# A two-layer decoder trunk: expert panels of 1,792 features, expert 0 gathered first, down weights in longer runs

## The reference, cut to what matters

```python
def swiglu(x, w_gate, w_up, w_down):
    return (jax.nn.silu(x @ w_gate) * (x @ w_up)) @ w_down

def moe_swiglu(x, w_router, w_gate, w_up, w_down):
    logits = (x @ w_router).astype(jnp.float32)
    top_vals, top_idx = lax.top_k(logits, TOP_K)          # TOP_K = 2
    weights = jax.nn.softmax(top_vals, axis=-1)
    ...                                                    # combine: weights by expert
    for e in range(N_EXPERTS):                             # 8, each 1024 x 3584 (x 3)
        out = out + combine[..., e:e + 1] * swiglu(x, w_gate[e], w_up[e], w_down[e])
    return out
...
        h = layer_norm(ALPHA * h + f, ln_g[i, 1], ln_b[i, 1])
        h = h + jax.nn.sigmoid(h @ ple_w_gate[i] + ple_b_gate[i]) * (p[i] @ ple_w_proj[i])
```

## Time and profile before

| | |
|---|---|
| median of 3 runs | 1474.14 us (1472.51 to 1475.07) |
| profiled execution, as timed | 1470.26 us |
| its span | 1468.5 us |
| TensorE (PE) busy | 1412.5 us, 96% |
| VectorE busy | 702.5 us, 48% |
| ScalarE busy | 319.8 us, 22% |
| GpSimd busy | 24.6 us, 2% |
| DMA | 467.99 MB, mean 319 GB/s; 130,864 packets on SyncE's queue q1 |
| ring products, gate and up (L1781) | 5,632 instructions |
| ring products, down (L1781) | 3,472 instructions |
| SiLU (L1054), hidden product (L1699) | 88 each, of 224 columns |
| turns (L1707) | 352, of 224 columns |

### The profile page before, as it was taken

The page is one execution under the profiler, slowest core; times in us unless marked ns, Lnnn a source line. Parts: engine busy times, 40 slices in busy tenths (PEclk is TensorE's granted clock), DMA queues, the critical chain, the costliest instruction groups (busy, mean ns, idle before and its releaser), DMA issues.

```text
span 1468.5 us, 27721 instructions
## 1 busy us (share of the span) xinstructions
PE 1412.5 (96%) x12131; PEld 925.5 (63%) x12131; DVE 702.5 (48%) x1128; ACT 319.8 (22%) x432; POOL 24.6 (2%) x51
## 2 busy tenths in 40 slices
PE   8999999999999999999999999999999999999687
PEld 7888788888778877356666664456454454465135
DVE  4795678878874668432332332241422322323247
ACT  4444344344455553000000000000000000000012
POOL 3010000000000000000000000000000000000100
PEclk9999999999999999999999999999999999999998
DMA  9956445555456126999999999999999999999980
GB/s 367 337 197 248 165 172 183 189 200 185 166 177 207 50 78 262 419 412 404 416 414 419 420 419 420 419 418 421 419 419 420 419 420 419 420 420 415 417 348 30
DMA packets 135481, 467.99 MB, mean 319 GB/s; under 512 B 8524, under 2 KB 9376, under 8 KB 134848
## 3 DMA queue, kind: packets, MB, share of 16 engines
q1 hardware_dynamic: 130864, 450.92, 77.9%
q0 software_dynamic: 2992, 12.70, 2.3%
q10 hardware_dynamic: 1504, 2.62, 0.5%
HBM read 462.53 MB, written 3.67 MB: 317 GB/s over the span
## 4 chain that ended last, share of the span: by engine, by line
PE 78%; DMA 13%; DVE 5%; ACT 2%; issue 1%; SPq 1%; POOL 0%; ACTq 0%; POOLq 0%; DVEq 0%
PE ps L1781 76%; DMA ring<-in_moe_w_up_dram 10%; DMA ring<-in_moe_w_down_dram 2%; DMA raw<-in_ple_w_gate_dram 1%; DVE split L1121 1%; PE ps L1799 1%; ACT split L751 1%; DVE h L1169 1%; DVE stats L1173 1%; DVE acc L1164 1%; DVE htl L1136 0%; SPq L578 0%; PE ps L2116 0%; PE ps L2152 0%; DVE acc L1216 0%
## 5 line engine op out<-in xcount | busy, mean ns | idle before, releaser
L1781 PE MATMUL ps<-ring,xt 128*32 128x448 f32 x5632 | 546.2, 542 | 25.9 <-DMA ring<-in_moe_w_up_dram 25.6
L1781 PEld LDWEIGHTS ps<-ring,xt 128*32 128x32 f32 x5632 | 256.7, 110 | 300.0 <-issue 242.1
L1781 PE MATMUL ps<-split,hth 128*128 128x512 f32 x1168 | 366.7, 395 | 6.0 <-DVE htl L1136 2.8
L1699 DVE TENSOR_TENSOR m_hb<-ps,m_sg 128x224 f32<-128x224 f32 x88 | 29.2, 385 | 575.8 <-ACT m_sg L1054 575.8
L1781 PE MATMUL ps<-ring,m_bt 128*32 128x256 f32 (+1 forms) x3472 | 278.4, 469 | 6.8 <-DMA ring<-in_moe_w_down_dram 6.7
L1781 PEld LDWEIGHTS ps<-split,hth 128*128 128x128 f32 x1168 | 218.9, 190 | 53.8 <-DVE htl L1136 3.4
L1781 PEld LDWEIGHTS ps<-ring,m_bt 128*32 128x32 f32 x3472 | 173.0, 110 | 108.7 <-issue 28.8
L1781 PE MATMUL ps<-split,htl 128*128 128x512 f32 x584 | 229.3, 393 | 0.0
L1707 DVE STREAM_TRANSPOSE m_bt<-m_hb 32x224 f32<-32x224 f32 x352 | 205.1, 583 | 5.5
L1054 ACT ACTIVATE m_sg<-ps 128x224 f32<-128x224 f32 x88 | 25.4, 357 | 727.7 <-PE ps L1781 727.7
L1121 DVE TENSOR_TENSOR split<-raw,split 128x2048 fp32r<-128x2048 f32 x52 | 118.7, 2291 | 64.0 <-ACT split L751 63.9
(11 more groups left out here) (256 smaller groups left out, 651.1 us busy)
## 6 DMA issues: line engine op xcount, KB each, us to landing
ring<-in_moe_w_gate_dram SPq DMA_DIRECT2D x128, 896.0 KB, 17.2
ring<-in_moe_w_up_dram SPq DMA_DIRECT2D x128, 896.0 KB, 16.6
ring<-in_moe_w_down_dram SPq DMA_DIRECT2D x128, 896.0 KB, 16.2
raw<-in_gm_w_in_dram SPq DMA_DIRECT2D x14, 1024.0 KB, 14.6
raw<-in_ffn_w_gate_dram SPq DMA_DIRECT2D x14, 1024.0 KB, 5.0
raw<-in_ffn_w_up_dram SPq DMA_DIRECT2D x14, 1024.0 KB, 5.0
raw<-in_ffn_w_down_dram SPq DMA_DIRECT2D x14, 1024.0 KB, 5.0
raw<-in_fox_w_in_dram SPq DMA_DIRECT2D x12, 1024.0 KB, 4.9
```

What stands on the lines that cost most here:

```text
L1699: ins = nc.vector.tensor_tensor(m_hb[:, q, :], ps[bank][:, QTR:2 * QTR], m_sg[:, q, :], ALU.mult)
L1781: return nc.tensor.matmul(o, a, b, start=start, stop=stop)
```

## The change

Panels have 1,792 features: 16 blocks, 24 slots each, one slot now holding one 128-row piece of gate or of up in one run of 7,168 bytes. All eight pieces of gate come first and then all eight of up, in banks of their own, 448 columns wide, and each slot is freed by itself. The up products of a wide panel use bank 0 of the gate products, after SiLU. A down transfer fills two slots in one run of 14,336 bytes and has a semaphore of its own. The order of blocks is expert 0 (2), three wide, one narrow, three wide, one narrow, four wide, two narrow. The hidden product is written over `m_sg`, `m_bt` has one buffer (and another for the last block), and so SiLU waits for the turns of the block before, and the turns wait for the down products of the block before.

`xh` and `xl` have room outside the ring and are made during routing. Expert 0's one-hot is made from `slots_e` before the sort, its gather (32 products of 96 columns) goes first, and the rest of the gather follows gate and up of block 0. The first 16 slots are filled in the order of `FILL`, the last three wait for `lg_full` only. Behind the experts the four gate pieces have a part of `split1` each, ScalarE's casts stand between the norm's steps, GpSimd takes the differences, the Sqrt table is loaded ahead, and the gate products go tile by tile. Code for a second round changes alike and is left out. In the diff `gate_rest` is GpSimd's, `wait_ge(bt_ready, ...)` is ScalarE's ahead of SiLU of block b, `select_first` and `turn_hidden` are VectorE's, `gate_up` and `gather_rest` TensorE's.

```diff
-PANEL = 896
+PANEL = 1792
...
-    SLOT = 2 * PANEL
-    X_BLK = 12
+    SLOT = PANEL
+    X_BLK = 24
...
-        between = len(few) - (NPAN - 1)
+        between = len(few) - NPAN
...
+    FIRST_BANKS = (3, 5)
+    REST_BANKS = (2, 3, 5)
+    def gate_banks(b):
+        return (0, 1) if narrow(b) else (0, 1, 4)
+    def up_banks(b):
+        return (6, 7) if narrow(b) else (6, 7, 0)
...
-    ADD_AT = {len(ORDER) - 2: (0, 1), len(ORDER) - 1: (2, 3)}
+    ADD_AT = {len(ORDER) - 1: (0, 1, 2, 3)}
...
+    FILL = (0, 1, 2, 3, 4, 5, 10, 11, 12, 6, 7, 8, 9, 13, 14, 15)
...
-                sp.wait_ge(gx_full, 2 * KD)
+                sp.wait_ge(lg_full, T)
...
+        for n in FILL:
+            ring_space(n)
             ring_load(n)
+        sp.wait_ge(placed, 1)
+        find_experts()
+        for n in range(RING, N_RING):
+            if not second_half(n):
+                sp.wait_ge(streams[0]["used"], G_MOE + n - RING + (2 if second_half(n + 1) else 1))
+            ring_load(n)
...
+                    if n == down_at(b) + 2 * i:
+                        sp.dma_start(ring[:, slot:slot + 2].rearrange("p (a s) n -> p a (s n)", a=1),
+                                     expert_rows(moe_w_down, e, j, i))                            .then_inc(down_landed[i] if b < NB - 1 else landed, 16)
...
+        def gate_rest(n):
+            pool.wait_ge(streams[1]["hi"], n + 1)
+            pool.tensor_tensor(split1[:, n, 1], raw[:, n], split1[:, n, 0].bitcast(F32), ALU.subtract)\
+                .then_inc(streams[1]["lo"], 1)
...
+                if b or r is not None:
+                    act.wait_ge(bt_ready, hid0 + b)
...
+        nc.scalar.activation(std[:, 0:1], var[:, 0:1], ACT.Sqrt)
         unfold_last()
-        round_hi(0, 1)
-        round_hi(1, 1)
+        gate_hi(0)
         norm_sqrt(1, 0, 1)
+        gate_hi(1)
+        gate_hi(2)
         tile_hi(0, 1)
-        round_hi(2, 1)
         norm_sqrt(1, 1, 1)
+        gate_hi(3)
         tile_hi(1, 1)
-        ple(1, 0, 3, 4)
+        last_ple()
...
+        def select_first(slot):
+            for m in range(T):
+                ins = nc.vector.tensor_scalar(every[:, m, 0, :], iota[:, 0:CAP], slot(m), None, ALU.is_equal)
+            ins.then_inc(every_ready, 1)
...
             def turn_hidden(b):
                 dve.wait_ge(e_hid, hid0 + (b + 1))
+                if 0 < b < NB - 1:
+                    dve.wait_ge(s0["used"], used0 + (G_MOE + down_at(b - 1) + 8))
...
             def gate_up(b):
+                for which, banks in enumerate((gate_banks(b), up_banks(b))):
+                    for k in range(KD):
+                        slot = landed(b, gu_at(b) + which * KD + k)
                         for q, bank in enumerate(banks):
+                            if which == 1 and k == 0 and bank in gate_banks(b):
+                                pe.wait_ge(e_silu, silu0 + (3 * b + gate_banks(b).index(bank) + 1))
                             for t in range(4):
...
+                                last = mm(ps[bank][t * G3:(t + 1) * G3, 0:QTR], xt[:, e // 4, k, tok:tok + G3],
+                                          ring[:, slot, quarter * QTR:(quarter + 1) * QTR], k == 0, k == KD - 1)
+                        last.then_inc(s0["used"], 1)
...
                     gate_up(b)
+                    if b == 0:
+                        pe.wait_ge(route_ready, 1)
+                        gather_rest(at_e, gx0)
```

More of the change, by code:

```diff
@@ L732, in _ @@
             gather_rows(2 * T, 1 + TABLE - CUT)
+        for n in range(4):
+            gate_rest(n)
     @block.scalar
@@ L891, in projected, with ple @@
                     .then_inc(proj_copied, 1)
-        def ple(which, g0, ready, last):
-            st = streams[which]
+        def ple(g0, ready, last):
+            st = streams[0]
             for nb in range(2):
@@ new lines, in ple @@
+                part = slice(nb * W, (nb + 1) * W)
+                dve.wait_ge(st["used"], g0 + 2 + 2 * nb)
+                for m in range(T):
+                    nc.vector.tensor_tensor(sig[:, m, part], ps[2 * (1 - nb) + m][:, :], ple_b[:, 0, part], ALU.add)\
+                        .then_inc(st["gb"], 1)
+                for m in range(T):
+                    dve.wait_ge(st["gs"], nb * T + m + 1)
+                    seq(nc.vector.tensor_tensor(sig[:, m, part], sig[:, m, part], pp[:, m, part], ALU.mult))
@@ new lines, in gather_expert_0 @@
+        def gather_expert_0(x_at, at_e):
+            pe.wait_ge(xh_ready, x_at)
+            pe.wait_ge(xl_ready, x_at)
+            pe.wait_ge(every_ready, at_e)
+            for k in range(KD):
+                o = ps[FIRST_BANKS[k // 4]][:, k % 4 * CAP:(k % 4 + 1) * CAP]
+                for x in (xh, xl):
+                    for m in range(T):
+                        last = mm(o, x[:, m, k * P:(k + 1) * P], every[:, m, 0, :], x is xh and m == 0,
+                                  x is xl and m == T - 1)
+                if k % 4 == 3:
+                    last.then_inc(gx_full, 1)
@@ new lines, in gather_rest @@
+        def gather_rest(at_e, gx0):
+            for n in range(2 * KD):
+                half, k = n // KD, n % KD
+                if k == 0:
+                    pe.wait_ge(every_ready, at_e + (half + 1))
+                if n >= 3:
+                    pe.wait_ge((gx_act, gx_dve)[(n - 3) % 2], gx0 + (2 + (n - 3) // 2))
+                e0 = 4 * half if half else 1
+                o = ps[REST_BANKS[n % 3]][:, 0:(4 * half + 4 - e0) * CAP]
+                for x in (xh, xl):
+                    for m in range(T):
+                        one = every[:, m, e0:4 * half + 4, :].rearrange("p e s -> p (e s)")
+                        last = mm(o, x[:, m, k * P:(k + 1) * P], one, x is xh and m == 0, x is xl and m == T - 1)
+                last.then_inc(gx_full, 1)
```

460 lines of the change are left out of this document (210 added, 250 removed).

## The result

The changed kernel takes 1484.45 us (median of 4 runs, 1483.52 to 1486.01), the kernel before on the same chip 1474.61 (4 runs, 1472.51 to 1475.67): ratio 1.0068, 95% interval 1.0053 to 1.0083. It is 10 us slower. The forecast was 1464.4, with 1459 to 1476 as the range and 0.12 for slower: wrong, and on the wrong side. The profiled execution took 1483.97 us, its span is 1482.2 where the forecast said 1458.8.

The account below looks back on a forecast made before the run. It took TensorE to set the pace up to the first narrow panel and the DMA from there to the last weight; -5.6 us (last slot earlier) and -4.1 (tail) summed to -9.7, median 1464.4, range 1459 to 1476.

Parts of the forecast that it names:

- Tail: From the last slot's products to the end: 4.1 us gained, with GpSimd taking the differences at 4.4 us each.
- R3: Rival, no change: a GpSimd difference takes 6.6 us, the fourth comes 7.2 us late; median 1471.6; chance 0.08.
- Head: Routing to block 0: expert 0's gather starts at 573.2 and takes 4.1 us; gate products begin at 578.1, before at 584.02.
- First narrow panel: Expert stage, after five wide panels: starts at 842.3; at the old pace the last slot is used 3.8 us later.
- The landing: Time from a ring transfer's issue to its arrival, at the first narrow panel: 6.5 us, between 4.6 and 8.3.
- Rate: Weight transfers from the first narrow panel on: longer runs save 0.0366 us a slot, 9.4 us over 256 slots.
- R2: Rival, no change: the weights' transfer rate doesn't move and landing stays at 8.3 us; median 1475.6; chance 0.14.
- Panels: Wide panels: VectorE's 12 turns take 14.0 us at 1.17 each, hidden behind TensorE's work, 4.8 us to spare.
- R1: Rival, slower: VectorE's turns don't fit in the wide panels; at 1.95 us each, 18.4 us, median 1482.8; chance 0.12.

Follow-up runs that it names:

- tail_dve: The changed kernel with the four differences of the last gate weights on VectorE between the token tiles, none on GpSimd: 1477.78 us, 1.0035 of the kernel before.
- both: The changed kernel with the differences back on VectorE (tail_dve) and 58 filler products (warm): 1471.04 us, 0.9990 of the kernel before.
- warm: The changed kernel with 58 instead of 26 filler products ahead of the wait for the experts' membership: 1477.02 us, 1.0033 of the kernel before.
- before_pool: The kernel before, with only the four differences of the last gate weights moved from VectorE to GpSimd: 1479.36 us, 1.0045 of the kernel before.
- gate3584: The kernel both, with each gate and up slot issued as two transfers in runs of 3,584 bytes: 1478.42 us, 1.0042 of the kernel before.
- down7168: The kernel both, with each two-slot down transfer issued as two of one slot, 7,168 bytes per run: 1473.57 us, 1.0004 of the kernel before.
- best: The kernel both with early2's panel order, hybrid's differences, and tile 1's turns behind all tile 0 gate products with more filler: 1460.42 us, 0.9914.
- early2: The kernel both, with the narrow panels as blocks 1, 6, 14 and 15 instead of 5, 9, 14 and 15: 1463.16 us, 0.9933 of the kernel before.
- hybrid: The kernel both, with the first and fourth difference on GpSimd beside VectorE's sums out of PSUM: 1470.76 us, 0.9988 of the kernel before.
- early: The kernel both, with the narrow panels as blocks 1, 6, 11 and 15 instead of 5, 9, 14 and 15: 1472.06 us, 0.9999 of the kernel before.
- newton: The changed kernel, with the last norm's Newton step as three VectorE instructions with one tensor input and per-partition scalars: 1474.09 us, one run.

## Why the prediction was wrong, by its own steps

*Tail.* This is the step that failed. It read that VectorE "loses two differences of 2.28 us between the tiles", priced GpSimd's operation at 4.4 us, and asked only whether the fourth would come in time. The price was right (4.53 to 4.71), and R3, which doubted it, is out. But it took GpSimd and VectorE for two engines that work side by side, and put the overlap's cost at nothing. The differences cost VectorE 9.1 us when it takes them and 14.2 us of stalls when GpSimd does. Of the 12.1 us, 5.0 (tail_dve) to 6.3 (both, 1416.58 to 1461.90, 45.3 us) go when VectorE takes them back. The rest, 5.8 us in both, is a gain that rested on VectorE being free: it fits TensorE's wait of 4.37 us for tile 1 and the 5 us at a granted clock of 0.66 behind it. The rule stands in the Trainium skill, "SBUF — State Buffer", section "SBUF: two separate sides": GpSimd and VectorE share one pair of SBUF ports, and whichever of a GpSimd instruction that reads SBUF and a VectorE one with two SBUF inputs is first keeps the other out for its whole length. The trace agrees in all four stalls (2.40, 4.15, 4.42 and 5.05 us, each up to the end of a GpSimd operation), and in what isn't stalled (0.15 to 0.75 us). I cited GpSimd's price list and missed this rule, which spoke against the change. The kernel before had no large GpSimd operation beside the norms, so its trace does not show this: with such a gap the offload needed a rival with a price, "as dear as on VectorE, or dearer".

*Head.* The start (573.3 against 573.2), the rest of the gather (11.0 us against 11.2) and all that follows block 0 were right. The gather of expert 0 was put at 4.1 us within 3.2 to 5.6 and took over 7, because every duration was taken at the full clock and here it was 0.50. The step itself moved 2.4 us of differences ahead of the routing, and so the wait for `member_b` grew: 0.1 us before (569.01 to 569.11), 2.01 after. warm shows both halves, 3.8 us for the gather at 1.00 and 36.29 for the block. It cost 5.2 us by the ratio. All nine profiled kernels with the 58 filler products have 1.00 from 560 to 595; of the three with the changed head and 26, one has 0.50, one 0.68 to 0.84 and one 1.00. The kernel before isn't safe from it either: before_pool, whose head is the same, has 0.86 and 0.80 in the windows from 570 to 580, behind 2.09 us of idle TensorE.

*First narrow panel.* Right at the full clock: 841.1 in warm, forecast 842.3. The landing was mis-sized, 6.5 us against a median of 8.7 for those asked for between 740 and 840 (slots freed singly don't land sooner, had 8.3): 2.2 us.

*Rate.* Right in size and cause, shown by gate3584 and down7168. The estimate from the Trainium skill, "DMA: Bandwidth & Descriptors", section "Why small descriptors are slow (HBM only)", was 6.1 us; the runs gave 9.8. R2 is out, though its other half, the landing that stays as it was, came true. In all, a slot took 2.218 us in the changed kernel and not 2.210: 1.9 us over 256, of which no run shows the cause.

*Panels.* Right: 168 turns of 952 ns, less than the 1.17 us that I took, and all hidden; no wait of TensorE for ScalarE in the wide panels. R1, the slower rival, is out too. The time came out on its side by something that no rival named.

The 1.9 us ahead of the change belong to that execution. Of the twelve later traces eight stand within 0.4 us of the kernel before at this mark, and four are 1.3 to 1.7 us late (best, down7168, early2, before_pool). One of the four is the kernel before with another tail, so the change is not the cause. What the cause is stays open.

## What to carry over

Work given to another engine is free only if that engine shares nothing with the one that it leaves: ask of each VectorE instruction beside it whether both of its tensor inputs lie in SBUF, and give GpSimd its work while VectorE reads PSUM (in hybrid such a sum kept its 0.75 us, though the gain was too small to be told). Whoever moves work ahead of a wait of TensorE lengthens that wait, and what follows may run at half the clock; look at the granted clock of the windows behind every idle stretch that the change makes longer, and put filler there. And a gain in the weights' stream counts only up to the next wait: early used them 12.6 us earlier, and gave all of it back to a wait for gathered rows.

## What was not expected of the hardware

- A VectorE instruction on one number per partition (0.16 us alone) took 4.42 us beside a GpSimd difference of 2,048 columns; between two GpSimd instructions just one held VectorE instruction got through (4.15 us, then 4.42; in newton 3.94, then 4.99). It seems to go the other way too: two GpSimd differences in a row took 9.03 us with a 128x1 instruction held between them, and 9.50 (newton) and 9.43 (before_pool) with one of 128x512.
- The granted clock fell to 0.50 for some 13 us (574 to 587) behind idle stretches of 1.07 and 2.01 us in one execution, and stayed at 1.00 behind the same stretches in another (newton).
- Behind the issue of three row gathers (1360 to 1363 in both, 1.57 MB) a ring slot took 3.4 us (products at 1371.03 and 1374.46) instead of 2.15. The rate did not fall, 429 GB/s from 1364.5 to 1376.8: a slot and a gather of 0.52 MB together are 1.44 MB, 3.4 us at 425 GB/s, an estimate.
